# A three-stage transformer kernel: recurrence output by token rows with moving states, and other products placed in front of TensorE's waits

## The chip, the cores and the metric

The kernel runs on one core of a Trainium2 chip. The metric is device time in microseconds (us) of one execution. All arithmetic is in 32-bit floats.

## The reference, cut to what matters

Two blocks follow each other on 256 tokens of width 1024. The first has a bidirectional gated linear attention (GLA) over chunks of 64 tokens, a pooling branch and a mixture of 32 experts; the second is two layers that mix a gated delta rule, a sparse attention and a gated linear recurrence ("hgrn2"), then a gated FFN. What the change touches:

```python
# GLA, per head (4 heads, 128 key and 256 value channels), per chunk of 64 tokens and direction
o_n   = q_n @ state                       # q_n = q * exp(cum), 64 x 128; state 128 x 256
state = d_n[..., None] * state + k_n.T @ v_n
o     = o_intra + o_inter                 # scores @ v inside the chunk, forward + backward
# output of the mixer
o = _rmsnorm(o, gla_onorm_g)              # mean of squares over the 256 value channels of a head and token
y_gla = (o * silu(g)) @ w_gla_br

# second block, delta rule
qkv = silu(causal_depthwise_conv(concat[q, k, v]))
q, k = l2norm(q), l2norm(k)               # sums of squares over the 128 channels of a head
u     = u0_c - w_c @ state                # per chunk
state = state * gl_c + k_dec.T @ u
# second block, hgrn2: scores inside a chunk, computed in three levels of block size
A = einsum(q_c, k_c, exp(b_c - b_s))
```

## The kernel before

There is no tile framework: each engine has a hand-written program, and semaphores order them. TensorE (`@block.tensor`) fills PSUM banks in rotation: `ph.bank(pe, key)` takes the next bank of the phase and waits until its last user freed it; `tiles(ph, key, parts, K)` (L591) writes one bank; `ph.freed(engine, key)` waits until the reader of `key` has freed its bank; `ph.read(engine, key)` waits until TensorE has filled it. In the trace a product of 32-bit floats is two MATMUL instructions, each with a weight load of its own, and a transpose is one. In "128\*64 128x512" the first pair is the stationary tile (contracted rows \* output partitions) and the second the moving tile (rows x columns).

**Stage 1, GLA.** For each head h of four (L770 to L810), TensorE makes the key-value products of the chunks ("kv", L781), two tiles of a gate projection ("gate", 32 instructions), and the output "o". It is held in transposed form: value channels on the partitions, tokens along the columns. So value tile `vt`, token tile `t` first gets the product inside the chunks (L799: stationary `vtok`, moving the scores `scT`, 128 columns), and then for each of two chunks and two directions the product of the state with the decayed queries (L807: stationary the state `st`, 128 wide, moving `qd`, 64 columns). ScalarE copies "o" to `oT` (L1750), and after the last head squares all of it (L1753, `osq`). After the two gate tiles of `project("gate", 2)` TensorE sums the squares over the channels with a matrix of ones ("oms", four heads by two channel tiles). ScalarE makes the reciprocal root of that (L1760, L1764), and VectorE, after its pooling work (L2269 to L2293), multiplies `oT` by it (L2298), then by the norm's weights and the gate `sg` (L2302), and signals `og_ready`. TensorE meanwhile does `project("gate", 3)`, the pooling products "yp" and "pbr", and then needs `oT` for "gbr". SyncE issues the router's weights and the first loads of expert weights after `og_ready` and "yp".

**The expert stage** streams 2 MB slabs through the six slots of `ring`; a slot's next load is issued when TensorE has read it (`w1_read`, `w3_read`, `y_full`).

**Each of the two layers.** VectorE makes the convolutions of q ("aq"), then k ("ak"), and signals `conv_ready`; ScalarE takes the SiLU of both at once (L1895) and their squares (L1896) and signals `qkv_steps`; TensorE, after "av" tile 0, waits for that and sums the squares in four banks ("l2", 16 instructions, the first wait at L1134). Later comes the chunk loop (L1227 to L1254), n = 0 to 3: "wS" n (w @ state), a wait until VectorE has subtracted it from `u` (L2728), "dS" n (k_dec.T @ u), then for n = 0 a filler projection, for n > 0 the score products "hs" of level n - 1, and for n = 1, 2 another filler. A filler is 32 instructions and does not depend on the loop. VectorE updates the state after "dS" (L2736) and then masks the scores (L2711, L2715).

Of the kernel before, what the change touches and what calls it, by code (L numbers as in the profile page):

```python
# [7 lines left out]
ALU = mybir.AluOpType  # L8
ACT = mybir.ActivationFunctionType
F32 = mybir.dt.float32  # L10
I32 = mybir.dt.int32
AX = mybir.AxisListType


P = 128
# [49 lines left out]
    "qkv_steps": 2, "l2_ready": 1,  # L65
    "dt_steps": 3,
    "AT_ready": 2, "B_ready": 12, "DT_arg": 2, "Gc_ready": 1, "MT_ready": 1, "Sh_ready": 1, "X0T_ready": 2,
    "conv_ready": 2, "down_read": 4, "down_first": 4, "first_copied": 4, "fg_ready": 1, "g_ready": 1,
# [78 lines left out]
def build(nc, W, out):  # L147
    offs, _ = constants()
    ctx = ExitStack()
    with ctx:  # L150
# [12 lines left out]
        def C(name):  # L163
            a, n = offs[name]
            return cst[:, a:a + n]
# [56 lines left out]
        def S(name):  # L222

            return sem(name)
# [45 lines left out]
        def due(name, n=1):  # L270

            return PER_LAYER[name] * ph3.layer + n + AHEAD.get(name, 0)
# [60 lines left out]
        osq = cum_flat[:, 2048:4096].rearrange("p (j t) -> p j t", j=KT)  # L333
# [23 lines left out]
        lastc = small[:, 48:52]  # L357

# [224 lines left out]
        def _(pe):  # L583
# [192 lines left out]
            for h in range(GH):  # L776
                for n, group in enumerate(KV_UNITS):
                    b = ph1.bank(pe, ("kv", h, n))
                    for d, c in group:
                        r = slice(CH * (c % 2), CH * (c % 2) + CH)  # L780
                        last = mm(PS[:, b, d * 256:(d + 1) * 256], krt[r, d, c // 2, h * P:(h + 1) * P],  # L781
                                  vtok[r, 2 + c // 2, h * 256:(h + 1) * 256], start=True, stop=True)
                    last.then_inc(psum_full, 1)

                w = slab("gate", h // 2)
                tiles(ph1, ("gate", h // 2, h % 2), [(slice(i * T, (i + 1) * T),
                                                      lambda k, f=2 * (h % 2) + i: w[:, k, f * P:(f + 1) * P], hx)
                                                     for i in range(2)], KT)
                last_unit1[where1[("gate", h // 2)]] = ("gate", h // 2, h % 2)

                pe.wait_ge(S("sc_ready"), h + 1)
                for n in (2, 3):
                    ph1.freed(pe, ("kv", h, n))
                b = ph1.bank(pe, ("o", h))
                for vt in range(2):
                    for t in range(TT):
                        o = vt * T + t * P
                        vs = slice(h * 256 + vt * P, h * 256 + (vt + 1) * P)
                        mm(PS[:, b, o:o + P], vtok[:, 2 + t, vs], scT[:, h, t, :], start=(vt == 0 and t == 0),  # L799
                           stop=False, skip_group_check=True)  # L800
                        for c in (2 * t, 2 * t + 1):
                            for d in range(2):
                                n = c if d == 0 else NCH - 1 - c
                                st = (s0[:, d, h, vt * P:(vt + 1) * P] if n == 0 else
                                      Sx[:, h % 2, d, n - 1, vt * P:(vt + 1) * P])
                                oo = o + CH * (c % 2)
                                last = mm(PS[:, b, oo:oo + CH], st, qd[:, d, h, c * CH:(c + 1) * CH],  # L807
                                          start=False,
                                          stop=(vt == 1 and c == NCH - 1 and d == 1), skip_group_check=True)
                last.then_inc(psum_full, 1)  # L810
            project("gate", 2, "gate", hx)
            pe.wait_ge(S("osq_ready"), 1)
            for hp in range(2):
                tiles(ph1, ("oms", hp), [(slice(i * T, (i + 1) * T), lambda k: C("ones"),
                                          lambda k, h=2 * hp + i: osq[:, 2 * h + k, :]) for i in range(2)], 2)
# [216 lines left out]
            for l in range(LAYERS):  # L1032
# [129 lines left out]
                pe.wait_ge(S("qkv_steps"), due("qkv_steps", 2))  # L1162
# [63 lines left out]
                for n in range(NCH):  # L1226
                    t, r_ = n // 2, slice(CH * (n % 2), CH * (n % 2) + CH)  # L1227
                    if n:
                        ph3.freed(pe, ("dS", n - 1))
                        tiles(ph3, ("wS", n), [((r_, slice(i * P, (i + 1) * P)),  # L1230
                                                lambda k, i=i: wk[:, i, n * CH:(n + 1) * CH],
                                                lambda k, i=i: Sd[n - 1][:, i, :]) for i in range(DNH)], 1)
                        ph3.freed(pe, ("wS", n))
                    if n < NCH - 1:
                        tiles(ph3, ("dS", n), [(slice(i * P, (i + 1) * P), lambda k, i=i: kd[r_, t, i, :],
                                                lambda k, i=i: u[r_, t, i, :]) for i in range(DNH)], 1)
                    if n == 0:
                        filler(0)
                        pe.wait_ge(S("qk_levels"), due("qk_levels", 2))
                    else:  # L1240
                        lv = n - 1
                        for par in range(2):
                            r_ = slice(64 * par, 64 * par + 64)
                            tiles(ph3, ("hs", lv, par), [
                                (slice((2 * i + t) * P, (2 * i + t + 1) * P),
                                 lambda k, i=i, t=t: args[r_, lv, 1, i * T + t * P:i * T + (t + 1) * P],
                                 lambda k, i=i, t=t: args[r_, lv, 0, i * T + t * P:i * T + (t + 1) * P])
                                for i in range(2) for t in range(TT)], 1)
                        if n == 1:
                            filler(1)  # L1250
                            pe.wait_ge(S("kdec_ready"), due("kdec_ready", 1))
                            turn("hkt", [eR[:, i, at(t)] for t in range(TT) for i in range(2)])
                        elif n == 2:
                            filler(2)  # L1254
# [373 lines left out]
        def _(act):  # L1628
# [118 lines left out]
            for h in range(GH):  # L1747
                gate_sigmoid(h // 2, h % 2)
                b = ph1.read(act, ("o", h))
                A(oT[:, 2 * h:2 * h + 2, :], PS[:, b, :].rearrange("p (j t) -> p j t", j=2),  # L1750
                  ACT.Copy).then_inc(psum_free[b], 1)
            ph1.freed(act, ("o", GH - 1))
            A(osq, oT, ACT.Square).then_inc(S("osq_ready"), 1)  # L1753
            for g in range(2):
                gate_sigmoid(2, g)
            orstd = e1.rearrange("p h t -> p (h t)")
            log_exp_table()
            for hp in range(2):
                b = ph1.read(act, ("oms", hp))
                A(orstd[:, hp * 512:(hp + 1) * 512], PS[:, b, :], ACT.Ln, scale=1.0 / 256, bias=C("eps"))\  # L1760
                    .then_inc(psum_free[b], 1)
            for hp in range(2):
                ph1.freed(act, ("oms", hp))
            A(orstd, orstd, ACT.Exp, scale=-0.5).then_inc(S("orstd_ready"), 1)  # L1764
# [75 lines left out]
            for l in range(LAYERS):  # L1840
# [53 lines left out]
                act.wait_ge(S("conv_ready"), due("conv_ready", 1))  # L1894
                link(A(cs[:, 0:8, :], cs[:, 0:8, :], ACT.Silu))  # L1895
                A(sc3[:, :, :], cs[:, 0:8, :], ACT.Square).then_inc(S("qkv_steps"), 1)  # L1896
# [6 lines left out]
                act.wait_ge(S("conv_ready"), due("conv_ready", 2))  # L1903
# [169 lines left out]
        def _(dve):  # L2073
# [169 lines left out]
            dve.wait_ge(S("dec_ready"), 1)  # L2243
            for h in range(GH):
# [19 lines left out]
                update(1, 2).then_inc(psum_free[banks[3]], 1)  # L2264

# [29 lines left out]
            dve.wait_ge(S("orstd_ready"), 1)  # L2295
            orstd = e1
            o4 = oT.rearrange("p (h v) t -> p h v t", h=GH)
            link(V.tensor_tensor(o4, o4, orstd.unsqueeze(2).broadcast_to([P, GH, 2, T]), ALU.mult))  # L2298
            for j in range(2):
                ph1.freed(dve, ("g", j, 1))  # L2300
            for j in range(KT):
                ins = V.scalar_tensor_tensor(oT[:, j, :], oT[:, j, :], colA("gla_onorm_g", j % 2), sg[:, j, :],  # L2302
                                             ALU.mult, ALU.mult)
            ins.then_inc(S("og_ready"), 1)
# [166 lines left out]
            for l in range(LAYERS):  # L2471
# [90 lines left out]
                for g in range(2):  # L2562
                    conv_tile(0, "aq", g)

# [472 lines left out]
```

## Time and profile before

| | |
|---|---|
| median of three runs | 1761.18 us (1760.28 to 1763.32) |
| the profiled execution: time, span of its trace | 1759.73 us, 1757.9 us |
| TensorE busy | 1706.7 us, 97% |
| VectorE busy | 716.9 us, 41% |
| ScalarE busy | 353.9 us, 20% |
| GpSimd busy | 82.1 us, 5% |
| expert weights: 96 loads of 2 MB | DMA engines full from about 400 us to about 830 us |

The busy shares say which engine the time is to be looked for on. They are means over stages with different limits, so the rows of a stage decide what an edit there is worth. A row of the timeline gives the start, the length of the merged piece, the engine, the line, output and inputs, and the count of instructions; a bracket at its end is idle time just before it and who ended it. Ends of matmuls are modelled, so neighbouring pieces overlap a little.

### The profile page before, as it was taken

What the parts mean: (1) busy time and instruction counts of PE and PEld (TensorE: products, weight loads), DVE (VectorE), ACT (ScalarE), POOL (GpSimd) and SP (SyncE); (2) the same over time, 40 slices, a digit from 0 to 9 for tenths busy, and PEclk for the clock granted to TensorE, in tenths of its full rate; (3) what the DMA queues carried; (4) which work ended last, traced back from release to release, by engine and by line L of the source; (5) the groups of instructions that cost most, each with busy time, mean ns of one, the idle gap of its engine ahead of it and who ended that gap; (6) DMA issues with size and microseconds to landing.
All of it is one profiled execution on the core that took longest, in us unless ns stands there. A gap on an engine that the chain in (4) does not pass through costs nothing.

```text
span 1757.9 us, 25380 instructions
## 1 busy us (share of the span) xinstructions
PE 1706.7 (97%) x10900; PEld 1321.6 (75%) x10900; DVE 716.9 (41%) x1369; ACT 353.9 (20%) x599; POOL 82.1 (5%) x94
## 2 busy tenths in 40 slices
PE   6999999999999999999999999999999999999998
PEld 3438898875454545454798989999899898999988
DVE  3308423151111111110278544776146944478712
ACT  2014211030000000000124322132011522223311
POOL 1200000000000000000102110100000211010000
PEclk9999999999999999999999999999999999999999
DMA  9873222729999999999443022454434212335541
GB/s 378 286 277 120 96 96 96 286 100 403 428 427 427 429 428 426 429 427 428 159 144 117 29 96 97 144 177 160 168 116 144 97 49 96 97 125 164 177 159 48
DMA packets 116858, 375.80 MB, mean 214 GB/s; under 512 B 12730, under 2 KB 62242, under 8 KB 101280
## 3 DMA queue, kind: packets, MB, share of 16 engines
q1 hardware_dynamic: 115380, 373.54, 55.3%
q8 instruction: 71, 1.16, 0.3%
q0 software_dynamic: 1216, 0.89, 0.2%
q14 instruction: 19, 0.16, 0.0%
q10 hardware_dynamic: 172, 0.05, 0.0%
HBM read 373.41 MB, written 1.05 MB: 213 GB/s over the span
## 4 chain that ended last, share of the span: by engine, by line
PE 74%; DMA 17%; DVE 6%; issue 1%; POOL 1%; ACT 1%; SPq 0%; DVEq 0%; POOLq 0%
PE PS L591 21%; DMA ring<-in_moe_w_dram 15%; PE PS L1398 13%; PE PS L941 8%; PE PS L1452 6%; PE PS L1363 3%; PE PS L687 3%; PE PS L1338 3%; PE PS L1473 2%; PE PS L841 2%; PE PS L972 2%; PE PS L1053 1%; DVE arena L2517 1%; DMA ring<-in_w_in_dram 1%; PE PS L626 1%
## 5 line engine op out<-in xcount | busy, mean ns | idle before, releaser
L591 PE MATMUL PS<-arena,ring 128*128 128x256 f32 (+1 forms) x1344 | 311.3, 392 | 3.2 <-DMA ring<-in_w_in_dram 2.2
L591 PEld LDWEIGHTS PS<-arena,ring 128*128 128x128 f32 x1344 | 254.3, 191 | 54.8 <-issue 17.8
L941 PE MATMUL PS<-ring,arena 128*64 128x512 f32 x1024 | 225.2, 594 | 7.9 <-DMA ring<-in_moe_w_dram 6.8
L1398 PE MATMUL PS<-arena,ring 128*128 128x128 f32 x2016 | 226.1, 275 | 0.0
L1398 PEld LDWEIGHTS PS<-arena,ring 128*128 128x128 f32 x2016 | 225.9, 192 | 0.2
L941 PEld LDWEIGHTS PS<-ring,arena 128*64 128x64 f32 x1024 | 74.2, 137 | 155.7 <-issue 155.7
L972 PE MATMUL PS<-ring,arena 128*64 128x512 f32 x512 | 113.4, 596 | 0.5 <-ACT arena L1816 0.5
L1452 PE MATMUL PS<-arena,ring 128*128 128x256 f32 x512 | 111.5, 379 | 0.0
L1452 PEld LDWEIGHTS PS<-arena,ring 128*128 128x128 f32 x512 | 96.9, 190 | 12.8
L2435 DVE TENSOR_TENSOR arena<-arena,PS 128x512 f32<-128x512 f32 x16 | 16.8, 1053 | 215.5 <-PE PS L941 215.5
L591 PE MATMUL PS<-arena 128*128 128x128 f32 (+3 forms) x704 | 87.4, 282 | 6.8 <-issue 3.5
L591 PEld LDWEIGHTS PS<-arena 128*128 128x128 f32 (+2 forms) x704 | 82.8, 188 | 11.7 <-issue 4.6
L972 PEld LDWEIGHTS PS<-ring,arena 128*64 128x64 f32 x512 | 35.3, 137 | 69.7 <-issue 68.9
L2831 DVE TENSOR_TENSOR ring<-ring 128x1024 f32<-128x1024 f32 x72 | 86.8, 1221 | 2.2 <-DMA ring<-in_ffn_w_up_dram 1.4
L914 PEld LDWEIGHTS PS<-arena 128*128 128x128 f32 x512 | 58.4, 192 | 13.1 <-issue 12.2
L2856 DVE SCALAR_TENSOR_TENSOR arena<-arena,colsL 128x255 f32<-128x255 f32 (+1 forms) x144 | 63.1, 480 | 1.9
L914 PE MATMUL PS<-arena 128*128 128x128 f32 x512 | 61.4, 279 | 0.1
L1363 PE MATMUL PS<-arena,ring 128*128 128x128 f32 x512 | 58.2, 275 | 0.0
L920 PE MATMUL PS<-arena 128*128 128x256 f32 x256 | 58.0, 380 | 0.0
L1363 PEld LDWEIGHTS PS<-arena,ring 128*128 128x128 f32 x512 | 57.7, 192 | 0.0
L591 PE MATMUL PS<-ring 128*128 128x256 f32 (+3 forms) x328 | 54.9, 358 | 1.7 <-DVE arena L2728 1.7
L1338 PE MATMUL PS<-arena,ring 128*128 128x128 f32 x448 | 51.5, 276 | 2.3 <-DVE arena L2770 2.3
(417 smaller groups left out, 1854.3 us busy)
## 6 DMA issues: line engine op xcount, KB each, us to landing
ring<-in_moe_w_dram SPq DMA_DIRECT2D x96, 2048.0 KB, 16.4
ring<-in_w_in_dram SPq DMA_DIRECT2D x23, 2048.0 KB, 9.1
ring<-in_ffn_w_up_dram SPq DMA_DIRECT2D x44, 1024.0 KB, 7.1
ring<-in_w_mod_dram SPq DMA_DIRECT2D x24, 1024.0 KB, 10.0
ring<-in_ffn_w_down_dram SPq DMA_DIRECT2D x10, 2048.0 KB, 7.9
ring<-in_w_out_dram SPq DMA_DIRECT2D x4, 2048.0 KB, 7.9
ring<-in_w_gla_br_dram SPq DMA_DIRECT2D x2, 2048.0 KB, 7.6
ring<-in_w_o_dram SPq DMA_DIRECT2D x2, 2048.0 KB, 8.4
```

The lines of the kernel that those rows point to most:

```text
L591: last = mm(PS[:, b, place] if not isinstance(place, tuple) else PS[place[0], b, place[1]], lhsT(k), rhs(k), start=(k == 0), stop=(k == K ...
L687: last = mm(PS[:, b, :], tokens[:, k, th(t)], weights[:, k, :], start=(first and k == 0), stop=(end and k == 3), skip_group_check=True)
L914: last = mm(PS[:, 6 + f // 4, (f % 4) * P:(f % 4 + 1) * P], h2t[:, t, f * P:(f + 1) * P], sel[:, t].rearrange("p e s -> p (e s)"), start=( ...
L920: return mm(PS[:, f // 2, (f % 2) * T:(f % 2 + 1) * T], ytok[:, f * P:(f + 1) * P], PT, start=False, stop=False, skip_group_check=True)
L941: last = mm(PS[e * SLOTS:(e + 1) * SLOTS, 4 + j, :], hg[:, k, e * SLOTS:(e + 1) * SLOTS], expert_slab(2 * j + e, KT)[:, k, :], start=(k == ...
L972: last = mm(PS[e * SLOTS:(e + 1) * SLOTS, 6 + n, :], hid[:, f, e * SLOTS:(e + 1) * SLOTS], expert_slab(4 + e, 4)[:, f, n * 512:(n + 1) * 5 ...
L1338: last = mm(PS[:, b, th(i)], w[:, k, th(i)], mixers(k)[:, th(t)], start=(t == 1 and k == 0), stop=(k == KT - 1), skip_group_check=True)
L1363: last = mm(PS[:, b, i * T + t * P:i * T + (t + 1) * P], w2[:, v, k, th(i)], second[t](k), start=(k == 0), stop=(k == KT - 1))
L1398: last = mm(PS[:, b, th(i)], w4[:, k, th(i)], b4[:, k, :], start=(first and i == 0 and k == 0), stop=(end and i == 1 and k == 3), skip_gro ...
L1452: last = mm(PS[:, banks[f // 2], half(f % 2)], w[:, k, f * P:(f + 1) * P], gated[:, j + k, :], start=(f % 2 == 0 and j + k == 0), stop=Fal ...
L2831: V.tensor_tensor(to[n - 1], a, b_, op).then_inc(S("weights_summed"), 1)
L2856: ins = V.scalar_tensor_tensor(dst[:, d:], src[:, 0:T - d], w[FFN_CONV - 1 - d], dst[:, d:], ALU.mult, ALU.add)
```

## The change

1. "o" is now held by token rows: for token tile `t`, the scores `scT` are stationary (128 wide) and `vtok` moves with 256 columns; then for each direction and chunk the decayed queries (64 wide) are stationary and the state moves with 256 columns, the output going to PSUM partitions 0 to 63 for an even chunk and 64 to 127 for an odd one.
2. ScalarE copies "o" to `otok` and squares it from PSUM. VectorE sums the squares along the row for each head, ScalarE makes the root of the 8 columns of sums, VectorE scales `otok` (8 operations) and signals `o_scaled`. TensorE then transposes `otok` (16 transposes, four banks "ot") after `project("gate", 2)`; VectorE multiplies straight from PSUM by the norm's weights and `sg`. "oms", the square over `oT` and the multiplication at L2298 go.
3. In each layer `conv_ready` is signalled after q and after k; ScalarE takes SiLU and squares of q, then of k; "l2" waits for q before its first bank and for k before its third.
4. In the chunk loop the products "hs" stand between "wS" and the wait for it, and every filler stands after "dS".

```diff
@@ TensorE, stage 1
+                for t in range(TT):
+                    place = slice(t * 256, (t + 1) * 256)
+                    mm(PS[:, b, place], scT[:, h, t, :], vtok[:, 2 + t, h * 256:(h + 1) * 256], start=(t == 0),
+                       stop=False, skip_group_check=True)
+                    for d in range(2):
+                        for c in (2 * t, 2 * t + 1):
+                            n = c if d == 0 else NCH - 1 - c
+                            st = s0[:, d, h, :] if n == 0 else Sx[:, h % 2, d, n - 1, :]
+                            r = slice(CH * (c % 2), CH * (c % 2) + CH)
+                            last = mm(PS[r, b, place], qd[:, d, h, c * CH:(c + 1) * CH], st, start=False,
+                                      stop=(c == NCH - 1 and d == 1), skip_group_check=True)
+                last.then_inc(psum_full, 1)
+            project("gate", 2, "gate", hx)
+            for h in range(GH):
+                pe.wait_ge(S("o_scaled"), h + 1)
+                b = ph1.bank(pe, ("ot", h))
                 for vt in range(2):
                     for t in range(TT):
+                        last = nc.tensor.transpose(PS[:, b, vt * T + t * P:vt * T + (t + 1) * P],
+                                                   otok[:, t, h, vt * P:(vt + 1) * P], C("ident"))
                 last.then_inc(psum_full, 1)
-            pe.wait_ge(S("osq_ready"), 1)
-            for hp in range(2):
-                tiles(ph1, ("oms", hp), ...)
@@ TensorE, layers
-                pe.wait_ge(S("qkv_steps"), due("qkv_steps", 1))
                 for g in range(4):
+                    pe.wait_ge(S("qkv_steps"), due("qkv_steps", g // 2 + 1))
...
+                        lv = n - 1
+                        for par in range(2):
+                            q_ = slice(64 * par, 64 * par + 64)
+                            tiles(ph3, ("hs", lv, par), ...)
                         ph3.freed(pe, ("wS", n))
                     if n < NCH - 1:
                         tiles(ph3, ("dS", n), ...)
+                        filler(n)
                     if n == 0:
-                        filler(0)
                         pe.wait_ge(S("qk_levels"), due("qk_levels", 2))
@@ ScalarE
+                by_tile = PS[:, b, :].rearrange("p (t v) -> p t v", t=TT)
+                A(otok[:, :, h, :], by_tile, ACT.Copy)
+                A(osq[h], by_tile, ACT.Square).then_inc(psum_free[b], 1)
+            log_exp_table()
+            act.wait_ge(S("osq_ready"), 1)
+            link(A(otok_rstd, otok_rstd, ACT.Ln, scale=1.0 / 256, bias=C("eps")))
+            A(otok_rstd, otok_rstd, ACT.Exp, scale=-0.5).then_inc(S("orstd_ready"), 1)
             for g in range(2):
                 gate_sigmoid(2, g)
...
+                for q_ in range(2):
+                    act.wait_ge(S("conv_ready"), due("conv_ready", q_ + 1))
+                    four = slice(4 * q_, 4 * q_ + 4)
+                    link(A(cs[:, four, :], cs[:, four, :], ACT.Silu))
+                    A(sc3[:, four, :], cs[:, four, :], ACT.Square).then_inc(S("qkv_steps"), 1)
@@ VectorE
+            def token_squares(h):
+                ph1.freed(dve, ("o", h))
+                return V.tensor_reduce(otok_rstd[:, h, :], osq[h], AX.X, ALU.add)
...
+            token_squares(GH - 1).then_inc(S("osq_ready"), 1)
+            dve.wait_ge(S("orstd_ready"), 1)
+            for h in range(GH):
+                for t in range(TT):
+                    ins = V.tensor_scalar(otok[:, t, h, :], otok[:, t, h, :], otok_rstd[:, h, t:t + 1], None, ALU.mult)
+                ins.then_inc(S("o_scaled"), 1)
... pooling work ...
+            for h in range(GH):
+                b = ph1.read(dve, ("ot", h))
+                for vt in range(2):
+                    j = 2 * h + vt
+                    ins = V.scalar_tensor_tensor(oT[:, j, :], PS[:, b, vt * T:(vt + 1) * T], colA("gla_onorm_g", vt),
+                                                 sg[:, j, :], ALU.mult, ALU.mult)
+            dve.sem_inc(S("og_ready"), 1)
```

## Rows read from the trace of the kernel before

**Rows 1.** The page: span, then busy time, share and instructions by engine.

```profile
span 1757.9 us, 25380 instructions
PE 1706.7 (97%) x10900; PEld 1321.6 (75%) x10900; DVE 716.9 (41%) x1369; ACT 353.9 (20%) x599; POOL 82.1 (5%) x94
```

**Rows 2.** TensorE's waits, whole execution: total us, times, longest us.

```profile
PE PS L591 <- DVE arena L2728: 5.0, 6, 0.9
PE PS L591 <- ACT arena L1896: 4.0, 2, 2.4
```

**Rows 3.** TensorE's timeline, stage 1: first head, then what follows the last.

```profile
208.38 1.57 PE L781 MATMUL PS<-arena 64*128 64x256 f32 x12
209.88 7.17 PE L591 MATMUL PS<-arena,ring 128*128 128x256 f32 x32
216.89 0.39 PE L799 MATMUL PS<-ring,arena 128*128 128x128 f32 x2
...
221.39 1.57 PE L781 MATMUL PS<-arena 64*128 64x256 f32 x12
...
274.22 3.62 PE L591 MATMUL PS<-ring,cst 128*128 128x256 f32 x16
277.67 13.98 PE L591 MATMUL PS<-arena,ring 128*128 128x256 f32 x64
```

**Rows 4.** TensorE's groups by shape, whole execution: busy us, mean ns | idle before.

```profile
L941 PE MATMUL PS<-ring,arena 128*64 128x512 f32 x1024 | 225.2, 594 | 7.9 <-DMA ring<-in_moe_w_dram 6.8 <-DVE arena L2426 1.1
L1062 PE MATMUL PS<-arena,ring 128*64 128x128 f32 x256 | 15.5, 277 | 0.1
L1197 PE MATMUL PS<-ring 128*64 128x256 f32 x32 | 5.7, 386 | 0.0
L739 PE MATMUL PS<-cst,ring 128*128 128x128 f32 x32 | 3.8, 273 | 0.0
```

**Rows 5.** Line L1197 by engine: ns min/median/max, first and last start, shape.

```profile
L1197 PEld LDWEIGHTS PS<-ring x32: 132/137/138, 988.5 to 1435.9; 128*64 128x64 f32 x32
L1197 PE MATMUL PS<-ring x32: 378/380/431, 988.5 to 1436.1; 128*64 128x256 f32 x32
```

**Rows 6.** ScalarE's timeline, stage 1: copy of the last "o".

```profile
260.55 0.60 ACT L1750 ACTIVATE ring<-PS 128x512 f32<-128x512 f32 x1 [3.81 <-PE PS L807]
```

**Rows 7.** VectorE's timeline, stage 1: pooling starts and ends, then L2302.

```profile
260.95 1.12 DVE L2269 MEMSET ring<- 128x1280 f32 x1 [9.04 <-PE PS L807]
...
268.65 1.22 DVE L2293 TENSOR_TENSOR ring<-ring,arena 128x1024 f32<-128x1024 f32 x1
...
282.08 3.26 DVE L2302 SCALAR_TENSOR_TENSOR ring<-ring,colsA,arena 128x256 f32<-128x256 f32 x8
```

**Rows 8.** DMA from 290 to 400 us, in 40 slices of 2.75 us: GB/s moved.

```profile
GB/s 2 299 402 66 0 0 0 265 404 93 0 0 244 402 173 241 435 441 417 447 417 441 220 0 0 161 399 209 77 328 357 0 0 3 6 0 0 0 0 298
```

**Rows 9.** ScalarE's timeline, layer 0: before and at the squares, and L1904.

```profile
921.73 1.28 ACT L1893 ACT_TABLE_LOAD   x1
926.87 1.91 ACT L1895 ACTIVATE arena<-arena 128x2048 f32<-128x2048 f32 x1 [3.86 <-DVEq L2582]
928.82 1.91 ACT L1896 ACTIVATE arena<-arena 128x2048 f32<-128x2048 f32 x1
...
950.76 1.06 ACT L1904 ACTIVATE arena<-arena 128x1024 f32<-128x1024 f32 x1 [2.78 <-DVEq L2625]
```

**Rows 10.** VectorE's timeline, layer 0: convolution ends of q and k, then the logits.

```profile
914.25 2.69 DVE L2517 SCALAR_TENSOR_TENSOR arena<-PS,colsL,arena 128x255 f32<-128x255 f32 x6
...
924.10 2.68 DVE L2517 SCALAR_TENSOR_TENSOR arena<-PS,colsL,arena 128x255 f32<-128x255 f32 x6
...
935.66 1.29 DVE L2602 TENSOR_TENSOR ring<-PS,ring 128x512 f32<-128x512 f32 x2 [2.21 <-PE PS L591]
```

**Rows 11.** TensorE's timeline, layer 0: "l2".

```profile
915.26 13.98 PE L591 MATMUL PS<-arena,ring 128*128 128x256 f32 x64
930.78 3.72 PE L591 MATMUL PS<-arena,cst 128*128 128x256 f32 x16 [1.54 <-ACT arena L1896]
```

**Rows 12.** TensorE's timeline, layer 0: chunk loop around n = 2.

```profile
1025.94 1.09 PE L591 MATMUL PS<-arena 128*64 128x128 f32 x8
1027.87 1.16 PE L591 MATMUL PS<-arena 64*128 64x128 f32 x8 [0.84 <-DVE arena L2728]
1028.86 1.61 PE L591 MATMUL PS<-ring 64*128 64x128 f32 x16
```

More of the change, by code:

```diff
@@ L332, in build @@
         oT = cum_flat[:, 0:2048].rearrange("p (j t) -> p j t", j=KT)
-        osq = cum_flat[:, 2048:4096].rearrange("p (j t) -> p j t", j=KT)
+        otok = cum_flat[:, 2048:4096].rearrange("p (t h v) -> p t h v", t=TT, h=GH)
+        osq = [w.rearrange("p h t -> p (h t)")[:, i * 512:(i + 1) * 512].rearrange("p (t v) -> p t v", t=TT)
+               for w in (e2, qT) for i in range(2)]
         pads = [qdki[:, i * 1280:(i + 1) * 1280].rearrange("p (g r w) -> p g r w", g=POOL_G, r=ROWS) for i in range(3)]
@@ L795, in _ @@
+                last.then_inc(psum_full, 1)
[3 more added lines that the diff above has]
+                b = ph1.bank(pe, ("ot", h))
                 for vt in range(2):
                     for t in range(TT):
[L797 to L809, printed above, removed]
@@ L1232, in _ @@
                                                 lambda k, i=i: Sd[n - 1][:, i, :]) for i in range(DNH)], 1)
+                        lv = n - 1
+                        for par in range(2):
+                            q_ = slice(64 * par, 64 * par + 64)
+                            tiles(ph3, ("hs", lv, par), [
+                                (slice((2 * i + t_) * P, (2 * i + t_ + 1) * P),
+                                 lambda k, i=i, t_=t_: args[q_, lv, 1, i * T + t_ * P:i * T + (t_ + 1) * P],
+                                 lambda k, i=i, t_=t_: args[q_, lv, 0, i * T + t_ * P:i * T + (t_ + 1) * P])
+                                for i in range(2) for t_ in range(TT)], 1)
                         ph3.freed(pe, ("wS", n))
@@ L1236, in _ @@
                                                 lambda k, i=i: u[r_, t, i, :]) for i in range(DNH)], 1)
+                        filler(n)
                     if n == 0:
-                        filler(0)
                         pe.wait_ge(S("qk_levels"), due("qk_levels", 2))
[L1240 to L1254, printed above, removed]
+                    elif n == 1:
+                        pe.wait_ge(S("kdec_ready"), due("kdec_ready", 1))
+                        turn("hkt", [eR[:, i, at(t_)] for t_ in range(TT) for i in range(2)])
                 ph3.freed(pe, "hkt")
@@ L2293, in _ @@
             V.tensor_tensor(pooled, pooled, hboth[:, 0:4, 0:T], ALU.subtract).then_inc(S("pooled_ready"), 1)
[L2295 to L2298, printed above, removed]
             for j in range(2):
                 ph1.freed(dve, ("g", j, 1))
[L2301 to L2304, printed above, removed]
+            for h in range(GH):
[4 more added lines that the diff above has]
+                                                 sg[:, j, :], ALU.mult, ALU.mult)
+                if h < GH - 1:
+                    ins.then_inc(psum_free[b], 1)
+            ins.then_inc(psum_free[b], 1)
+            ph1.freed(dve, ("ot", GH - 1))
+            dve.sem_inc(S("og_ready"), 1)
             for g in range(2):
@@ L2563, in _ @@
                     conv_tile(0, "aq", g)
+                dve.sem_inc(S("conv_ready"), 1)
                 b = ph3.read(dve, "G")
```

30 lines of the change are left out of this document (7 added, 23 removed).

## The prediction

> **What bounds the kernel now.** I read the page first. TensorE is busy 1706.7 of 1757.9 us [rows 1], so the time is what TensorE executes plus what it waits for, except where a stage has another limit. Next came the list of TensorE's waits. Two of its entries belong to this change: six waits of 5.0 us in all for VectorE's subtraction in the chunk loop, and two of 4.0 us in all for ScalarE's squares in front of "l2" [rows 2]. Last came the timeline of stage 1. From the first "kv" to the last gate tile no row of TensorE has an idle bracket [rows 3], so there only less work for TensorE can save time. There is one stage with another limit: the expert stage, where DMA is full. What matters for it is whether its stream starts earlier when TensorE does. In the last 25 us before 397 us DMA moves next to nothing, and the stream starts in the last slice, behind the first expert product [rows 8]. The stream hangs on TensorE's progress, so a gain made ahead of it moves it too.
>
> **Stage 1, "o".** Removed: a head's "o" runs from 216.89 to 221.39 us [rows 3], 4.50 us, and the pattern repeats four times: 17.9 us (40 instructions a head, 0.112 us each, whether they move 128 or 64 columns). Added, a head: 4 instructions with a full stationary tile and 256 moving columns, and 16 with a 64-wide stationary tile and 256 columns.
> - The full ones: "gate" has this shape, 32 instructions from 209.88 to 216.89 us [rows 3], 7.01 / 32 = 0.219 us each. 16 of them in all: 3.5 us.
> - The 64-wide ones, 64 in all: no row has this shape in this order, so I bound it. In L941 and L1062 the two halves of PSUM's partitions alternate, product by product, as they will here (even chunk, odd chunk). There an instruction of 512 columns costs 225.2 / 1024 = 0.220 us and one of 128 columns 15.5 / 256 = 0.061 us [rows 4]; between them, 256 columns cost about 0.110 us, which is half of the full tile's price: two halves run side by side. In L1197, of just this shape, eight instructions go to one half and then eight to the other; they cost 5.7 / 32 = 0.178 us [rows 4]. Without any overlap it would be 0.219 us. I take 0.110, by the rows whose order is the new one: 7.0 us. The ends are 7.0 and 14.0 us.
> - Changes between full and half tiles: three more a head. The first matmul of L1197 behind another form takes 431 ns where the median is 380 [rows 5], 0.05 us; and where a tile form changes, the next piece overlaps the last by 0.07 us (209.88 + 7.17 against no change: 217.05 against 216.89, 0.16 us; with a change: 208.38 + 1.57 = 209.95 against 209.88) [rows 3], another 0.09 us. Some of it is one and the same thing, so 0.12 us each for 12: 1.5 us (between 0 and 1.7).
>
> Here a rule speaks against the change. The rows put a change of form at 0.05 to 0.14 us. The Trainium skill (TensorEngine Tiling (Array Packing), Key Properties) says that changing the tiling mode, not just the tile, drains TensorE. A drain that let nothing overlap would cost the whole 0.16 us and the 0.05 us on the first matmul, 2.5 us for 12 where I take 1.5: the sum would be 1.0 us smaller.
>
> So "o" costs 3.5 + 7.0 + 1.5 = 12.0 us in place of 17.9: **-5.9 us**.
>
> **Stage 1, the norm.** "oms" goes: 274.22 to 277.67 us [rows 3], -3.45 us. 16 transposes come, 3.8 / 32 = 0.119 us each [rows 4]: +1.9. **-1.55 us.** Stage 1 together: -7.45 us, between -9.1 (no cost for changes) and -0.45 (no overlap of halves).
>
> What must be hidden: the new chain from "o" of the last head to `o_scaled`, with two new waits. Let its end be 0. ScalarE copies and squares, 2 x 0.60 us [rows 6], to 1.4. VectorE sums 512 elements; a reduction is at most what its other passes over 1024 elements cost, 1.22 us [rows 7]: 2.7. ScalarE's table and two operations on 8 columns, under 1.28 us for the table [rows 9] (loaded meanwhile) and 0.5 for the rest: 3.3. VectorE scales with 8 operations of 256 elements, at most 3.26 us like L2302 [rows 7]: 6.6. TensorE reaches the transposes behind two gate tiles, 14 us. Slack 7 us. Queued on VectorE behind the wait for the root: the pooling work, 260.95 to 269.87 us [rows 7], 8.9 us, so ready at 15.5; TensorE asks for it at 14 + 1.9 + 14 = 30. Then eight multiplications from PSUM, at most 3.5 us behind the last transpose: `og_ready` at about 20, needed at 45, and by SyncE's queue (router and expert loads) not before "yp" at 31. Queued on ScalarE behind its wait for the sums: the two gate tiles, whose banks are asked for again at 16 or later. If this cover were gone, TensorE would wait up to 6.6 us. The removed square over 2048 and multiplication at L2298 lay beside other work and give nothing.
>
> **Layers, "l2".** VectorE ends the convolution of q at 914.25 + 2.69 = 916.94 us and that of k at 926.78 [rows 10]. ScalarE's table is in at 923.01 [rows 9], so q's SiLU and squares (1.06 us each for 1024 elements [rows 9]) run from 923.0 to 925.2, before k is ready; k's run from 926.87 to 929.05 in place of 930.73. TensorE ends "av" at 915.26 + 13.98 = 929.24 [rows 11]. Its wait of 1.54 us goes, and so does the empty pipeline behind it: last start 928.86, next start 930.78, 1.92 us where 0.22 is the pace; -1.7 us. In layer 1 the wait is 2.4 us [rows 2]; there k's squares come 1.7 us earlier, and two banks of "l2" (1.9 us) stand in front of the wait for them: -2.6 us. What is late next: VectorE goes straight on from its convolutions to the logits, where it has 2.21 us of idle time [rows 10]. In layer 0 this takes the 1.7 us; in layer 1 it is short by some 0.3 us, which later slack before "kk" takes up. **-4.3 us.**
>
> **Layers, chunk loop.** After "wS" TensorE now goes on to "hs", 16 instructions and 1.5 us [rows 12], while VectorE subtracts in 0.85 us. The wait is covered three times a layer. From starts: last start of "wS" 1025.94 + 1.09 - 0.27 = 1026.76, next start 1027.87 [rows 12], 1.11 us where 0.2 remains with a change of form. The three are 0.85, 0.9 and 0.9: **-5.3 us** in two layers, between -5.0 (the waits alone) and -6.0. "hs" delays "dS" and so VectorE's state update, but the filler of 7 us behind "dS" now covers that, for n = 1 and 2; for n = 3 there is no "dS". "hs" of level 0 needs `qk_levels`, which TensorE already awaits at the same place.
>
> **Sum.** -7.45 - 4.3 - 5.3 = -17.05 us. The profiled execution took 1759.73 us with a span of 1757.9; that becomes 1742.7. The median of the runs lies 1.45 us above the profiled one: 1761.18 - 17.05 = **1744.1 us**.
>
> **Rivals.**
> - Halves do not overlap in runs of only eight instructions between full tiles: 0.219 us each, 7.0 us more: 1751.1. With L1197's 0.178: 4.4 us more, 1748.5. L1197 speaks for it, L941 and L1062 against it; there the alternation is the new one.
> - One of the layers' waits moves rather than goes: "l2" still waits for k, or VectorE falls behind at the logits. Price 4.3: 1748.4. Against it: k's squares at 929.05 against TensorE's 929.24, a close call, but two banks stand in front.
> - The expert stage takes the gain of stage 1, since its DMA stream sets its end. Price 7.45: 1751.6. Against it: DMA stands still before the stream starts [rows 8].
> - Weight loads of half tiles are exposed. What it would do: each of the 64 instructions costs 0.137 us of load [rows 5] plus 0.219: 22.8 us, 15.8 more than I take: 1759.9, within 0.2%. Against it: L1062 keeps 0.061 us an instruction, less than half of a load [rows 4]. The Trainium skill (TensorE: Matmul & The Clock Gate, Part 3) has the rule behind it: a weight load overlaps running matmuls only when the row group differs, and here both halves use all rows. By that rule, L1062 should be slower than it is; the trace disagrees.
> - Slower: half-tile products of one row group do not pipeline at all, 0.380 + 0.137 = 0.517 us each [rows 5], 33.1 us, 26.1 more: 1770.2. It decides from 0.110 + 17.05 / 64 = 0.376 us an instruction; nothing in rows 4 is near that, and L1197 runs this shape at less than half of it.
>
> **How the numbers follow.** A measurement of this kernel tells about 0.2% (3.5 us) from no change. Forecast as costed 0.76; less or no overlap of halves 0.08; a layer wait stays 0.06; the expert stage takes it 0.05; exposed loads 0.03; slower 0.02. The forecast's own range is 1741 to 1747: 1.65 us less if changes of form cost nothing and 0.7 if the loop gives 6.0, and up to 3 more for partly overlapping halves and for the drain. The range for 8 in 10 takes in the next cases: 1740.8 to 1751.1. Faster 0.95, same 0.03, slower 0.02.
>
> **What would show it.** In the profile after: "o" of one head about 3.0 us long, with 64-wide instructions at about 0.110 us; no idle time before the first transpose; "yp" asked for with no new wait; the first expert product some 7.5 us earlier, and the first product after the expert stage by the same amount; no wait of "l2" for L1896's successor in either layer; no wait of "dS" for VectorE's subtraction. Wrong it would be if "o" takes over 4 us, if TensorE waits before the transposes, or if the expert stage ends less than 7 us earlier.

## The result and the profile after

The kernel after takes 1744.57 us (median of four executions, 1743.09 to 1745.88) against 1760.73 for the kernel before (also four): a ratio of 0.9902, with a 95% interval from 0.9888 to 0.9917; the two medians themselves divide to 0.9908. 1744.1 us was predicted. The profiled execution took 1743.09 us, 16.6 less than that of before. Its page begins as follows (compare rows 1):

```profile
span 1741.2 us, 25246 instructions
PE 1698.5 (98%) x10820; PEld 1307.4 (75%) x10820; DVE 718.6 (41%) x1380; ACT 352.5 (20%) x605; POOL 82.2 (5%) x94
```

TensorE's work is 8.2 us less and its idle time 8.5 us less. To see where, I take points that both kernels pass. The chains of waits give those of the layers (start us, length us, piece); first before, then after:

```profile
867.15 10.76 PE PS L1053 x96
970.55 10.84 PE PS L591 x96
1046.42 1.84 PE PS L1288 x16
1315.93 7.15 PE PS L1053 x64
1415.70 10.84 PE PS L591 x96
1491.57 1.84 PE PS L1288 x16
```

```profile
859.44 10.76 PE PS L1056 x96
961.03 10.84 PE PS L594 x96
1034.21 1.84 PE PS L1287 x16
1303.71 7.15 PE PS L1056 x64
1401.68 10.84 PE PS L594 x96
1474.86 1.84 PE PS L1287 x16
```

The first and fourth piece of each list are a layer's query products ("query_part" in the kernel, L1053 before and L1056 after). Each pair of neighbours brackets one thing: the stretch with "l2" in it, then the levels of the scores and the chunk loop, then the rest of layer 0 with its FFN, and again for layer 1. With the timelines of stage 1 this gives:

| stretch | before, us | after, us | change | predicted |
|---|---|---|---|---|
| start of the first "kv" | 208.38 | 208.29 | -0.09 | 0 |
| from there to the end of the fourth "o" | 51.97 | 46.78 | -5.19 | -5.9 |
| to the start of `project("gate", 3)` | 17.32 | 15.67 | -1.65 | -1.55 |
| to the first expert product | 111.50 | 110.85 | -0.65 | 0 |
| to the query products of layer 0 | 477.98 | 477.85 | -0.13 | 0 |
| layer 0, "l2" in it | 103.40 | 101.59 | -1.81 | -1.7 |
| layer 0, chunk loop in it | 75.87 | 73.18 | -2.69 | -2.65 |
| to layer 1, FFN in it | 269.51 | 269.50 | 0 | 0 |
| layer 1, "l2" in it | 99.77 | 97.97 | -1.80 | -2.6 |
| layer 1, chunk loop in it | 75.87 | 73.18 | -2.69 | -2.65 |
| to the end | 266.33 | 266.34 | 0 | 0 |
| sum | | | -16.7 | -17.05 |

The timeline of TensorE in stage 1, after, which answers rows 3:

```profile
216.80 0.59 PE L800 MATMUL PS<-arena,ring 128*128 128x256 f32 x2
217.33 1.08 PE L807 MATMUL PS<-arena,ring 128*64 128x256 f32 x8
218.34 0.70 PE L800 MATMUL PS<-arena,ring 128*128 128x256 f32 x2
218.97 1.08 PE L807 MATMUL PS<-arena,ring 128*64 128x256 f32 x8
219.98 1.57 PE L784 MATMUL PS<-arena 64*128 64x256 f32 x12
...
268.99 1.91 PE L816 MATMUL PS<-cst,ring 128*128 128x128 f32 x16
270.74 13.98 PE L594 MATMUL PS<-arena,ring 128*128 128x256 f32 x64
```

A head's "o" goes from 216.80 to 219.98, 3.18 us where it was 4.50. Eight half-tile instructions (L807) take 1.01 us from their start to the next piece's, 0.126 us each. In front of the transposes (L816) there is no idle bracket. The chain that had to be hidden, on ScalarE and on VectorE (which answer rows 6 and 7), ran like this:

```profile
255.68 0.59 ACT L1751 ACTIVATE arena<-PS 128x512 f32<-128x512 f32 x1
...
257.92 0.21 ACT L1755 ACTIVATE small<-small 128x8 f32<-128x8 f32 x1
```

```profile
256.31 0.69 DVE L2243 TENSOR_REDUCE small<-arena 128x2 f32<-128x512 f32 x1 [7.85 <-ACT arena L1751]
258.16 2.19 DVE L2272 TENSOR_SCALAR ring<-ring,small 128x256 f32<-128x256 f32 x8 [1.17 <-ACT small L1755]
...
268.27 1.23 DVE L2302 TENSOR_TENSOR ring<-ring,arena 128x1024 f32<-128x1024 f32 x1
```

The last "o" ends at 255.07, the last scaling at 260.35, 5.3 us later (6.6 was my bound), and TensorE asks for it at 269. The pooling work is ready at 269.50 and asked for at 284.55.

### The profile page after: what moved, and what is told of

Same layout as the page of the kernel before. It is cut to its first block, busy times and chain, and to the rows that moved or that the text cites. A ratio compares the mean times of both kernels' runs of the same rounds, so it can differ in the third digit from the quotient of the medians.

```text
span 1741.2 us, 25246 instructions
## 1 busy us (share of the span) xinstructions
PE 1698.5 (98%) x10820; PEld 1307.4 (75%) x10820; DVE 718.6 (41%) x1380; ACT 352.5 (20%) x605; POOL 82.2 (5%) x94
## 4 chain that ended last, share of the span: by engine, by line
PE 80%; DMA 16%; DVE 2%; POOL 1%; issue 1%; ACT 0%; SPq 0%; DVEq 0%; POOLq 0%
PE PS L594 26%; DMA ring<-in_moe_w_dram 14%; PE PS L1397 13%; PE PS L944 8%; PE PS L1451 6%; PE PS L1362 3%; PE PS L690 3%; PE PS L1337 3%; PE PS L1472 2%; PE PS L975 2%; PE PS L844 2%; PE PS L1056 1%; DMA ring<-in_w_in_dram 1%; PE PS L917 1%; PE PS L923 1%; PE PS L629 1%
```

## The experiments

The kernels of "Stage 1 alone", "The layers alone", "Full tiles first" and "Both improvements" were executed four times each, all others once. So most of what follows is read from stretches of one trace. Stretches that an edit leaves alone repeat within 0.1 us: the one with "l2" in layer 0 takes 103.40 us before, 103.42 with stage 1 alone and 103.42 with the slower step.

**Stage 1 alone.** The kernel before with the edits of stage 1 (points 1 and 2 of the change), all its layers as they were.

> The kernel before with the change of stage 1 alone. My theory: the parts add up, since the expert stage's DMA stream starts when TensorE does. The first expert product (389.17 us before, 381.59 after) comes at 381.6, the layers keep their old lengths and waits, and the span is 7.6 to 7.8 us shorter than before, the same in the layers as ahead of them. Rival (the expert stage takes the gain): the first expert product is at 381.6, but the layers begin where they did, 860 us, and the time stays.

Measured: 1754.65 us, ratio 0.9954 (0.9937 to 0.9970). From the first "kv" to the transposes ahead of the second token tile's sums, shortly before the experts (L865 before, L868 after), it took 152.39 us, as in the kernel after, against 159.87 before: -7.5. Below, "stage 1" is this stretch. Its layers keep their lengths: 103.42 us for the stretch with "l2" in layer 0 (103.40 before). The experts took none of it: from the first expert product to layer 0's query products it is 477.93 us (477.98 before), and the kernel before took 1762.36 us beside these runs, 7.7 more. In the profiled execution the first expert product came at 383.8 us and not at 381.6: 0.5 us of this is a first "kv" that began later (208.82), 1.7 us is the clock, told in the last section.

**The layers alone.** The kernel before with points 3 and 4 of the change.

> The kernel before with the edits of the two layers alone. If the parts add up: stage 1 as before, first product of layer 0 at 861.7 us as before; layer 0 shorter by 4.5 us (1.8 at the squares of q and k, 2.7 in the chunk loop), layer 1 shorter by 4.5 (1.8 and 2.7): 9.0 in all. Rival (the layers gain only because stage 1 moved something, for example the bank rotation): less than 8.

Measured: 1751.89 us, ratio 0.9938 (0.9921 to 0.9955). The stretches with "l2" take 101.60 us in layer 0 and 97.99 in layer 1, those with the loop 73.19 and 73.27: the values of the kernel after, within 0.1 us. Against before that is 8.9 us in all, so the rival ("less than 8") falls. The point at which layer 0 was expected, 861.7 us, was a slip: its query products begin at 867.15 us before and began at 869.48 here, behind a first "kv" 0.7 us later and 1.4 us lost by the clock. Together the two halves of the change give 0.9954 x 0.9938 = 0.9892, and the whole gave 0.9902: the parts add, within the intervals.

**The bank rotation.** The table has 0.65 us that no edit of the diff was meant to give. Before, the first output projection of stage 1 (L841) stood idle for 0.83 us, and started just after VectorE had read the last bank that it had to free (L2321, done at 336.80):

```profile
336.90 4.37 PE L841 MATMUL PS<-arena,ring 128*128 128x128 f32 x37 [0.83 <-issue]
```

```diff
+            for i in range(2):
+                ph1.at[("skipped", i)] = None
             project("gate", 3, "gate", hx)
```

> The kernel before with nothing but PSUM's rotation of the first phase moved on by two banks ahead of the third gate projection, as the change does by taking four banks for the transposed output where it took two for the sums. My theory for the 0.65 us that stage 1 gained beyond its own edits: the first output projection took the bank that VectorE had to free last. Then the 0.83 us of idle time in front of L841 shrinks to 0.2 here too and the first expert product comes 0.65 us earlier, at 388.5 us, with no other difference. Rival: it came from VectorE or the weight slabs being early. Then 389.2 stays.

Measured, TensorE's timeline at that place:

```profile
336.83 1.50 PE L843 MATMUL PS<-arena,ring 128*128 128x128 f32 x12
338.50 2.72 PE L843 MATMUL PS<-arena,ring 128*128 128x128 f32 x22 [0.17 <-DVE arena L2326]
```

Twelve instructions now run before the projection waits, and it waits 0.17 us for its operand instead of 0.83 for its bank. Stage 1 takes 159.25 us in place of 159.87: 0.62 us. The first expert product came later than expected, at 391.2 us, by the clock effect of the last section and a "kv" that began 0.9 us late, so the time of the whole execution says nothing here. The stretch does: the gain came from four banks taken where two had been, by accident.

**Full tiles first.** Two products with full tiles, then all eight with half tiles.

```diff
                 for t in range(TT):
                     place = slice(t * 256, (t + 1) * 256)
                     mm(PS[:, b, place], scT[:, h, t, :], ...)
+                for t in range(TT):
+                    place = slice(t * 256, (t + 1) * 256)
                     for d in range(2):
```

> The kernel after, but in each head's output both products with a full stationary tile come first and then all eight with half tiles (16 instructions in a row): two changes of tile form fewer. In the kernel after a head takes 3.18 us: 0.88 for the four full instructions, 1.76 for sixteen half ones at 0.110, and 0.54 left over. My theory: what is left over hangs on the changes of form and on runs as short as eight. Then a head takes 2.8 to 2.9 us and the four save 1.1 to 1.5 us. Rival (a half-tile instruction of 256 columns simply costs 0.126 us wherever it stands, 1.01 us for eight): 3.1 us a head, 0.3 us in all.

```profile
216.75 1.03 PE L800 MATMUL PS<-arena,ring 128*128 128x256 f32 x4
217.70 1.95 PE L809 MATMUL PS<-arena,ring 128*64 128x256 f32 x16
219.58 1.57 PE L784 MATMUL PS<-arena 64*128 64x256 f32 x12
```

A head takes 2.83 us (216.75 to 219.58), 0.35 less, and the 16 half-tile instructions 1.88 us, 0.118 each. The price per instruction falls with the length of the run, as the first theory says. Stage 1 is 151.00 us in place of 152.39. Eight half-tile instructions more in the same run add 0.87 us (1.88 - 1.01), 0.109 each, which is the 0.110 that was taken. Two changes of form with the shorter runs that go with them cost 0.35 us, 0.17 each, where I had 0.12; the run takes both away at once and does not tell them apart. The ratio to the kernel before is 0.9890 (0.9873 to 0.9906); this interval overlaps that of the kernel after, so the gain is shown by the stretch and not by the time.

**The order of the halves.** Both directions of the even chunk, then both of the odd one.

```diff
-                    for d in range(2):
-                        for c in (2 * t, 2 * t + 1):
+                    for c in (2 * t, 2 * t + 1):
+                        for d in range(2):
```

> The kernel after with the half-tile products in another order: both directions of the even chunk, then both of the odd one, so four instructions go to one half of PSUM's partitions and then four to the other. The price of 0.110 us that I took rests on alternation. If overlap needs it, the runs of eight (1.01 us after) grow to 1.3 to 1.5 us, a head from 3.18 to 3.8 to 4.2. If the engine overlaps halves in whatever order: 1.0 us and 3.18.

```profile
217.31 1.09 PE L807 MATMUL PS<-arena,ring 128*64 128x256 f32 x8
218.34 0.70 PE L800 MATMUL PS<-arena,ring 128*128 128x256 f32 x2
```

1.03 us for eight, against 1.01 when they alternate. My theory fell: the overlap does not need alternation, at least not in runs of four instructions to a half. In L1197, with eight to one half and then eight to the other, an instruction costs 0.178 us [rows 4]. No run here changed the order alone to eight and eight, so whether it is the order that makes L1197 dearer, and from which length on, stays open.

**One half only.** Every half-tile product goes to partitions 0 to 63.

```diff
-                            r = slice(CH * (c % 2), CH * (c % 2) + CH)
+                            r = slice(0, CH)
```

> The kernel after with all the half-tile products sent to partitions 0 to 63, so that nothing can run side by side; the state's part of the output is thereby wrong, and only stage 1 is to be read, since the experts' load may differ. It measures the price without overlap: 0.219 us an instruction, 1.8 us for eight, a head 4.8 us where the kernel before has 4.50. The rival of exposed weight loads would give 0.356 us an instruction, 2.8 us for eight.

```profile
217.95 1.94 PE L807 MATMUL PS<-arena,ring 128*64 128x256 f32 x8
219.82 0.70 PE L800 MATMUL PS<-arena,ring 128*128 128x256 f32 x2
```

Eight take 1.87 us, 0.234 each, and a head 4.89. So two halves side by side save 0.86 us in eight instructions, 6.9 us in all; without them "o" would be slower than before (4.89 us a head against 4.50), so the whole gain of that edit is this overlap. The rival of exposed weight loads (0.356 us) is far off.

**"l2" waits for k.** In layer 1 the change gave 1.80 us where I had 2.6. TensorE and VectorE, layer 1, after:

```profile
1361.13 3.62 PE L594 MATMUL PS<-arena,cst 128*128 128x256 f32 x16
1364.67 2.98 PE L594 MATMUL PS<-ring 64*128 64x256 f32 x16
1367.59 7.17 PE L594 MATMUL PS<-arena,ring 128*128 128x256 f32 x32
```

```profile
1363.79 2.68 DVE L2529 SCALAR_TENSOR_TENSOR arena<-PS,colsL,arena 128x255 f32<-128x255 f32 x6
1366.51 1.29 DVE L2615 TENSOR_TENSOR ring<-PS,ring 128x512 f32<-128x512 f32 x2
```

The wait of "l2" (L1896 before) is gone, but the logits' products behind it take 2.98 us where they took 2.10. Their last product takes the PSUM bank of v's first tile, which VectorE frees with its convolution, at 1366.47. To see whether this is what holds layer 1:

```diff
-                    pe.wait_ge(S("qkv_steps"), due("qkv_steps", g // 2 + 1))
+                    pe.wait_ge(S("qkv_steps"), due("qkv_steps", 2))
```

> The kernel after, but the sums of squares wait for k's squares before their first bank; ScalarE still works in two halves. In layer 1 the change gave 1.8 us where I had 2.6, and the piece of the logits' products behind it is 0.88 us longer. My theory: its last product takes the bank that VectorE's convolution of v's first tile frees, so TensorE cannot be earlier there anyway. Then layer 0 loses 0.1 to 0.2 us, layer 1 has a wait of 0.9 us in front of the sums and none in the logits' products, and its length stays. Rival (the logits' piece is slow for another reason): layer 1 loses 0.9 us.

```profile
1363.88 3.72 PE L594 MATMUL PS<-arena,cst 128*128 128x256 f32 x16 [0.84 <-ACT arena L1891]
1367.53 2.10 PE L594 MATMUL PS<-ring 64*128 64x256 f32 x16
```

0.84 us of idle time came back ahead of "l2", the logits' products are at 2.10 us again, and layer 1's stretch is 98.19 us, only 0.22 more than after (layer 0: 101.80, 0.21 more). The two waits stand for one another, as the theory says. It also shows what is worth what in this edit: nearly all of it is ScalarE's earlier work on q; TensorE's own earlier start gives 0.2 us a layer, as long as the logits' products wait for their bank in layer 1.

**Second logits later.**

```diff
-                for t in range(TT):
-                    pairs_by_rows("lg", qb, kbb, t)
+                pairs_by_rows("lg", qb, kbb, 0)
                 pair_of(w_av, ("av", 1), 256)
+                pairs_by_rows("lg", qb, kbb, 1)
```

> The kernel after with the logits' products of the second token tile behind v's second projection tile (7 us) in place of ahead of it. If the bank of VectorE's convolution is what holds them in layer 1, layer 1 gets 0.9 us shorter and layer 0 stays. If VectorE's chain as a whole is what bounds (logits, norms, then the products of k with k), the wait comes back ahead of those, and layer 1 stays as it is or gets longer.

```profile
939.20 0.60 PE L1032 MATMUL PS<-cst,arena 128*128 128x128 f32 x4
944.62 1.11 PE L1032 MATMUL PS<-cst,arena 128*128 128x128 f32 x4 [4.82 <-DVE arena L2529]
```

Both expectations missed: 1757.37 us, layer 0 6.8 us and layer 1 6.1 us longer. The wait is neither at the logits nor at the products of k with k, but at the transposes of k (L1032), for 4.82 us, until VectorE has convolved v's second tile. The move had changed which bank "av" 1 took. The phase has eight banks, and the second group of these transposes is the eighth allocation behind "av" 1, so it takes that very bank. It is the same mechanism in another place.

**A bank passed over.** The order is that of the kernel after again; only the rotation changes.

```diff
+                    if par:
+                        ph3.at[(ph3.layer, "skipped")] = None
                     tiles(ph3, ("lg", 1, par), ...)
```

> The kernel after with one PSUM bank passed over ahead of the last logits' product, so that it takes a bank that ScalarE freed long before, not the one that VectorE's convolution of v's first tile frees. The run before moved the products instead and gave their place in the rotation to v's second tile, whose late convolution then held the transposes of k for 4.8 us. If the bank is the cause: layer 1 shorter by 0.8 to 0.9 us, the logits' piece back at 2.10 us, layer 0 unchanged; the rotation of all later banks moves by one, which may cost some tenths. If VectorE's chain bounds: the 0.9 us comes back in front of the products of k with k.

```profile
1365.16 2.10 PE L594 MATMUL PS<-ring 64*128 64x256 f32 x16
```

The logits' products take 2.10 us, layer 1's stretch 97.08 us (-0.89), layer 0's 101.59 (unchanged), and no wait came back elsewhere. With it, this stretch of layer 1 gives 2.7 us in all, where 2.6 was predicted. The bank is the cause.

**A slower step in the chunk loop.** How much do the score products cover? One more VectorE pass ahead of each subtraction, in the kernel before and in the kernel after.

```diff
                         ur = u[r_, t].rearrange("p h c -> p (h c)")
+                        V.tensor_tensor(cat[r_, 0:2, :].rearrange("p k t -> p (k t)"), ur, ur, ALU.add)
```

> The kernel before with one more VectorE pass of 64x512 (about 0.69 us, into space that is free there) ahead of each subtraction in the chunk loop. Nothing covers the wait there: each of the six waits grows from 0.8 to about 1.5 us, each layer by 2.1, the time by 4.1.

> The kernel after with the same extra pass of about 0.69 us ahead of each subtraction. My theory: the score products (1.75 us from the last product of the state to the first behind them) cover 1.05 us of latency now and have 0.7 to spare. Then the wait in front of the state's update stays under 0.1 us each and a layer grows by less than 0.3. Rival (the gain came from the fillers' new place, and the score products cover nothing more): a layer grows by 1.4 or more.

Before, with the pass: the six waits grew from 5.0 to 10.1 us, but the stretch with the loop grew by 7.43 us in layer 0 and 7.47 in layer 1, where 2.1 was expected. TensorE's waits, and its clock in three 2 us stretches (PE, PEld, DVE, ACT and POOL busy, clock, DMA):

```profile
PE PS L591 <- DVE arena L2729: 10.1, 6, 2.0
```

```profile
1034.00:1036.00 2.00, 2.00 (x15) 2.00 (x17) 0.89 (x4) 0.00 (x0) 0.00 (x0) 0.73 0.03 8
1036.00:1038.00 2.00, 2.00 (x13) 1.78 (x13) 1.31 (x3) 0.00 (x0) 0.00 (x0) 0.50 0.00 0
1042.00:1044.00 2.00, 2.00 (x11) 1.77 (x10) 0.00 (x0) 0.00 (x0) 0.00 (x0) 1.00 0.00 0
```

The rows stand behind a wait of 1.45 us. There the granted clock is 0.50, which is 1.2 GHz, from about 1035.0 to 1041.6 us; behind the wait of 2.03 us in the turn before it is so from about 1021.4 to 1024.3. Behind the third wait, of 1.56 us, it stays at 1.00, and layer 1 shows the same three. So 5.1 us of added waiting cost 14.9 us in the loops, about 10 of them by the clock.

After, with the pass (layer 0, first two turns of the loop):

```profile
1005.85 1.71 PE L594 MATMUL PS<-ring 64*128 64x128 f32 x16
1007.94 1.16 PE L594 MATMUL PS<-arena 64*128 64x128 f32 x8 [0.39 <-DVE arena L2742]
...
1019.10 1.16 PE L594 MATMUL PS<-arena 64*128 64x128 f32 x8
```

The stretch grew by 1.58 us in each layer, 0.65, 0.41 and 0.52 us in the three turns of layer 0, where I expected under 0.3 a layer. The rival named 1.4 or more, and by that number it won. Its reason, that the score products cover nothing more, does not hold: the three passes took 1.23, 0.68 and 0.69 us, 2.60 in all, so 1.0 us of them was covered. What was wrong was my spare time of 0.7 us a turn, and the length of the first pass. In the first turn the spare is near that: VectorE is done at 1006.62 us in the kernel after and "dS" begins at 1007.38. In the second turn "dS" (the product that the state's update needs) begins not behind the score products but among them, at 1018.02 us, and VectorE is done at 1017.77: the spare is 0.25 us. The kernel says why the turns differ. The last score products have their operands on partitions 64 to 127, "dS" has them there in the first turn and on partitions 0 to 63 in the second, and the traces show pieces interleaved only in the latter case. In the kernel before it is the same, with "dS" 1 and the score products of partitions 0 to 63 behind it.

**Both improvements.**

> The kernel after with the full tiles first in each head and the bank passed over. If both effects hold and add: stage 1 shorter by 1.5 us as in the run with full tiles first, layer 1 by 0.9, together 2.4 us less than the kernel after (a ratio of about 0.989 to the kernel before).

Measured: 1742.05 us (1741.73 to 1742.98), ratio 0.9884 (0.9867 to 0.9900). Stage 1 is 151.00 us and layer 1's stretch 97.08, as in the runs with one of them: 1.39 + 0.89 = 2.3 us less than after, and the medians differ by 2.5. The intervals of the two ratios (0.9867 to 0.9900 here, 0.9888 to 0.9917 for the kernel after) overlap; the stretches of the profile are what shows the gain.

## Why the prediction was right

The direction, the bounds and the mechanisms held. That the sum came within 0.35 us of the profiled change (-16.7 for -17.05) is partly luck: "o" gave 0.7 us less than predicted and "l2" in layer 1 0.8 us less, and 0.65 us came unlooked for from the rotation of banks, with 0.5 us in small differences. The prediction also has a slip in its ends: it takes off 1.65 us for changes of form at no cost where its sum has 1.5, so -9.1 should be -8.95, and the low end 1741 should be about 1742.

**What bounds it** held: TensorE's work and waits, and the expert stage passed on what stage 1 gained. From the first expert product to layer 0's query products the two kernels differ by 0.13 us.

**"o"**: -5.19 where I had -5.9. The price of the full tiles held. The term that was mis-sized is the changes of tile form: I took 0.12 us each from rows 5 and the overlaps of rows 3; the run with the full tiles first gives 0.17, the shorter runs included. A head of 3.18 us leaves 0.54 us for all three, in place of 0.36, so the term is 2.2 us and not 1.5. The Trainium skill (TensorEngine Tiling (Array Packing), Key Properties) says that changing the tiling mode drains TensorE. I had put a full drain at 2.5 us for twelve changes; the measured 2.2 is nearer to that than to my choice. No run here shows whether a drain is what costs it.

**The halves' overlap**: right in size, 0.110 us as taken (0.109 for each of eight more in a row; 0.118 in the run of sixteen and 0.126 in runs of eight, with the entry into them), and the rivals of no overlap (0.234 measured) and of exposed loads fell. The reason that I gave was too narrow: I took the rows with alternation for it, and grouped halves do as well.

**The norm**: -1.65 for -1.55. The cover was 14 us, as worked out, and the chain 5.3, under the bound of 6.6. I missed that four banks in place of two move the rotation, 0.65 us; I had asked of banks only whether they are free in time, not which bank the next projection would get.

**"l2"**: layer 0 as predicted. In layer 1 I had seen that VectorE would be late next, by 0.3 us, and looked for it at the logits that VectorE reads. It showed where TensorE takes a bank that VectorE frees, 0.88 us. The step that failed is "later slack takes up": the products stood 0.88 us for the bank, and none of it came back. **The chunk loop**: 2.69 for 2.65, by starts and not by the idle brackets, whose sum (2.5 a layer) is less.

## What to carry to other kernels

Work out what a wait is worth from starts (the last one before it, the first one behind it, less the usual pace), and give changes of tile form a price of their own. With PSUM banks in rotation, each bank added, dropped or moved gives all later products another predecessor: list for each of them who frees its bank, and when. A free bank passed over can be worth as much as an edit.

## What the runs showed of the hardware

TensorE's clock fell behind waits of 1.5 to 2 us, and not each time. In each kernel of this case TensorE idles 1.70 and then 0.40 us some 17 us ahead of the first expert product, and the eight products behind it (L887 here) are the same. In the kernel after, and then in the one with stage 1 alone:

```profile
364.60 3.60 PE L887 MATMUL PS<-arena 128*128 128x512 f32 x8
```

```profile
365.13 5.29 PE L887 MATMUL PS<-arena 128*128 128x512 f32 x8
```

The second ran at a granted clock of 0.50 from 366 to 368 us, and lost 1.7 us. Of the profiled executions of 14 kernels, those of before, after and three others kept the clock there and nine lost it. 1.7 us is over half of the spread between executions of one kernel (1743.09 to 1745.88 us). The mean granted clock fits: the kernel after took 1743.09 and 1743.45 us with 0.998, and 1745.68 and 1745.88 us with 0.996. This is why single times are read by their stretches here. In the kernel before with the slower step, the waits of 2.03, 1.45 and 1.56 us in each loop brought the clock down twice, behind the first and the second, and cost more through it (about 10 us in two layers) than the 5.1 us by which the waits had grown.
